# One adaLN block at each of four edges of a decoder trunk, in place of ten pieces of each mixing part

## The reference

```python
mod = (jax.nn.silu(c) @ w_ada + b_ada).reshape(B, N_SUB, 3, D_MODEL)
m_shift, m_scale, m_gate = mod[:, :, 0], mod[:, :, 1], mod[:, :, 2]

def sub_in(t, i):
    return rmsnorm(t, norm_pre[i]) * (1.0 + m_scale[:, i, None]) + m_shift[:, i, None]

def sub_out(t, y, i, res):
    return t + res * m_gate[:, i, None] * rmsnorm(y, norm_post[i])

x = sub_out(x, swiglu(sub_in(x, 0), ffn_up[0], ffn_down[0]), 0, FFN_RES)
h = sub_in(x, 1)
pa, pb, pg = split_cols(h @ w_in, [A_COLS, B_COLS, 2 * D_MODEL])
...
x = sub_out(x, merged, 1, 1.0)
x = sub_out(x, swiglu(sub_in(x, 2), ffn_up[1], ffn_down[1]), 2, FFN_RES)
```

## Time and profile before

| | |
|---|---|
| runs | 2221.89, 2221.23 and 2217.05 us, median 2221.23 |
| the profiled execution | 2214.12 us |
| its span on the core | 2212.4 us |
| mean granted PE clock | 0.937 |
| PE busy | 2025.4 us, 92% |
| DVE, ACT busy | 57%, 43% |
| DMA, mean over the span | 160 GB/s |

### The profile page before, as it was taken

One profiled execution on the slowest core, in us unless ns is written; L12 is line 12 of the kernel. 1 busy time (PEld: TensorE's weight loads), 2 busy tenths in 40 slices (PEclk: granted clock), 3 DMA queues, 4 the chain that ended last, 5 costly groups with the idle time before them and its releaser, 6 DMA issues.

```text
span 2212.4 us, 44807 instructions
## 1 busy us (share of the span) xinstructions
PE 2025.4 (92%) x19104; PEld 1831.7 (83%) x19104; DVE 1256.2 (57%) x2161; ACT 954.3 (43%) x1872; POOL 4.8 (0%) x30
## 2 busy tenths in 40 slices
PE   6999989889999997899989998988899989879997
PEld 4899868778877877789989996888898878668997
DVE  3554455656456555677566645455654655558853
ACT  4333464444466413433454445433445752253343
POOL 0000000000000000000000000000000000000000
PEclk8999999999999887899999999888999988789998
DMA  7787755556555536697646655434545444167762
GB/s 255 219 233 200 196 143 153 160 143 183 132 161 149 155 83 149 165 254 221 193 121 181 181 174 142 127 107 129 134 108 143 108 120 124 51 160 220 229 192 93
DMA packets 579797, 353.33 MB, mean 160 GB/s; under 512 B 43989, under 2 KB 539639, under 8 KB 578047
## 3 DMA queue, kind: packets, MB, share of 16 engines
q1 hardware_dynamic: 490634, 302.74, 48.6%
q10 hardware_dynamic: 88964, 47.74, 8.7%
HBM read 332.27 MB, written 18.50 MB: 159 GB/s over the span
## 4 chain that ended last, share of the span: by engine, by line
PE 74%; DVE 9%; DMA 7%; ACT 6%; issue 3%; ACTq 2%; SPq 0%; DVEq 0%
PE bank L879 70%; DMA ring<-in_w_ada 3%; DMA ring<-in_ffn_up 2%; DVE ring_r L731 2%; DVE far L1904 1%; ACT w_hi_r L723 1%; DVE big L1904 1%; PE bank L644 1%; PE bank L657 1%; ACTq L570 1%; DVE big L1907 1%; ACTq L625 1%; ACT h L1448 1%; DVE big L606 1%; DVE far L1907 1%
## 5 line engine op out<-in xcount | busy, mean ns | idle before, releaser
L879 PE MATMUL bank<-big_r,w_hi_r 128*128 128x264 f32 x4160 | 1082.1, 294 | 54.4 <-DVE h_r L1904 41.0
L879 PE MATMUL bank<-big_r,ring_r 128*128 128x264 f32 (+1 forms) x3456 | 999.1, 289 | 0.0
L879 PEld LDWEIGHTS bank<-big_r,w_hi_r 128*128 128x128 f32 x4160 | 754.6, 193 | 127.1 <-issue 90.9
L879 PE MATMUL bank<-h_r,w_hi_r 128*128 128x264 f32 x2752 | 802.0, 291 | 0.0
L731 DVE TENSOR_TENSOR ring_r<-ring,w_hi_r 128x1024 fp32r<-128x1024 f32 (+2 forms) x440 | 524.4, 1195 | 477.6 <-ACT w_hi_r L723 473.7
L879 PEld LDWEIGHTS bank<-big_r,ring_r 128*128 128x128 f32 (+1 forms) x3456 | 668.5, 193 | 1.0
L723 ACT CAST w_hi_r<-ring 128x1024 fp32r<-128x1024 f32 (+2 forms) x440 | 452.1, 1028 | 498.5 <-PE bank L879 288.1
L879 PEld LDWEIGHTS bank<-h_r,w_hi_r 128*128 128x128 f32 x2752 | 535.5, 195 | 1.1
L879 PE MATMUL bank<-big,far 64*64 64x64 f32 (+2 forms) x1440 | 158.9, 268 | 0.0
L879 PEld LDWEIGHTS bank<-big,far 64*64 64x64 f32 (+1 forms) x1440 | 124.5, 144 | 7.2 <-issue 6.7
L879 PE MATMUL bank<-ring,c 128*32 128x256 f32 x1152 | 95.7, 411 | 27.8 <-DMA ring<-in_w_ada 19.7
(11 more groups left out here) (287 smaller groups left out, 1924.9 us busy)
## 6 DMA issues: line engine op xcount, KB each, us to landing
ring<-in_ffn_up SPq DMA_DIRECT2D x176, 512.0 KB, 4.7
ring<-in_w_in SPq DMA_DIRECT2D x148, 512.0 KB, 3.9
ring<-in_w_ada SPq DMA_DIRECT2D x144, 512.0 KB, 4.0
ring<-in_ffn_down SPq DMA_DIRECT2D x64, 512.0 KB, 3.8
far<-in_state_gdn_ssm ACTq DMA_DIRECT2D x28, 512.0 KB, 6.0
ring<-in_ffn_down SPq DMA_DIRECT2D x32, 384.0 KB, 3.2
ring<-in_w_out SPq DMA_DIRECT2D x16, 512.0 KB, 4.7
out_sample_gdn_ssm<-far ACTq DMA_DIRECT2D x16, 512.0 KB, 4.2
```

The lines of the kernel that those rows point to most:

```text
L879: return pe.matmul(out, lhsT, rhs, start=start, stop=stop)
```

## The change

Four blocks move to four edges: (0,0), (0,1), (0,2) and (1,0). At each, three units stand on PE right behind the first mean (`edge_begins`), the fourth behind the fifth product of the second mean, and the sum piece behind the second mean. ACT copies `ada_rows` between the seventh and the eighth square and `modv` after `normalise`. Both mixing parts lose ten pieces: layer 0 leaves out turns 1, 2, 6, 11, 16, 21, 26, 31, 36, 41 and 46 (turn 1 had none before), and layer 1 keeps those of turns 0, 2, 5, 7, 10 and so on, up to 72. The means go from bank 7, where the units write, to bank 0, and wait there for the eviction of the output tile before. In the plan the next part's first two tiles take the two oldest slots ahead of the edge's units. `weight_plan` is written anew and, but for this, gives the same order.

```diff
 def mix_pieces(l, turn):

     if l == 0:
-        return 1 if turn != 1 else 0
-    return 1 if turn % 2 == 0 or turn in (3, 5) else 0
+        return 0 if turn in (1, 2, 6, 11, 16, 21, 26, 31, 36, 41, 46) else 1
+    return 1 if turn % 5 in (0, 2) and turn < 75 else 0
+
+
+def edge_pieces(l, sub):
+
+    return ADA_UNITS + 1 if (l, sub) in ((0, 0), (0, 1), (0, 2), (1, 0)) else 0
...
+def ring_slots(plan, in_mixing, edges):

     ended, count = [-1] * RING, [0] * RING
-    slot, before, nth_load = [], [], []
-    for n, (_, kind, _) in enumerate(plan):
+    slot, before, nth_load = ([0] * len(plan) for _ in range(3))
+    order = list(range(len(plan)))
+    for n in edges:
+        order[n:n + ADA_UNITS + 2] = [n + ADA_UNITS, n + ADA_UNITS + 1, *range(n, n + ADA_UNITS)]
+    for n in order:
         own = range(RING)
         if n in in_mixing:
-            own = (RING - 1,) if kind == "ada" else range(RING - 1)
+            own = (RING - 1,) if plan[n][1] == "ada" else range(RING - 1)
         s = min(own, key=lambda s: ended[s])
...
-                    def mean_square(bank=7, buf=h):
-
+                    def mean_square(buf=h, sub=None):
+
+                        m, fill = (l, sub) if sub != 2 else (l - 1, 2), sub is not None
                         for k in range(NT):
                             pe.wait_ge(sq_ready.sem, sq_ready.next(pe))
-                            i = mm(banks[bank][:, 0:T], mean_all[:, :], buf[:, k, :], k == 0, k == NT - 1)
+                            i = mm(banks[0][:, 0:T], mean_all[:, :], buf[:, k, :], k == 0, k == NT - 1)
+                            if fill and k == 4 and edge_pieces(*m):
+                                ada_pieces(1)
                         i.then_inc(ss_done.sem, ss_done.one())
+                        if fill and edge_pieces(*m):
+                            ada_pieces(1)
+
+                    def edge_begins(sub):
+                        if edge_pieces(l, sub):
+                            ada_pieces(ADA_UNITS - 1)
...
-                        if l == 0:
-                            pe.wait_ge(ada_taken.sem, ada_taken.nth((ADA_FFN, ADA_MIX + ADA_FFN)[i_ffn]))
+                        pe.wait_ge(out_taken.sem, out_taken.at(base + 5))
                         mean_square()
+                        edge_begins(2 * i_ffn)
...
-                    def square_input(start=False):
+                    def square_input(start=False, m=None):
                         for j in range(NT):
                             if j == 0 or not start:
                                 act.wait_ge(x_ready.sem, x_ready.next(act))
                             act.activation(h[:, j, :], xT[:, j, :], ACT.Square).then_inc(sq_ready.sem, sq_ready.one())
+                            if m and j == 6 and edge_pieces(*m):
+                                ada_pieces(ADA_UNITS)
+                        if start:
+                            ada_pieces(ADA_UNITS)
+                        normalise()
+                        if m and edge_pieces(*m):
+                            ada_pieces(1)
```

More of the change, by code:

```diff
@@ L131, in mix_pieces, with units, edge @@
     if l == 0:
[L132 to L133 removed]
+        return 0 if turn in (1, 2, 6, 11, 16, 21, 26, 31, 36, 41, 46) else 1
+    return 1 if turn % 5 in (0, 2) and turn < 75 else 0
+def edge_pieces(l, sub):
+    return ADA_UNITS + 1 if (l, sub) in ((0, 0), (0, 1), (0, 2), (1, 0)) else 0
 def weight_plan():
[L138 to L139 removed]
+    steps = iter([key for m, b in ada_order() for key in ada_units(m, b, b + 1) + [None]])
+    def units(n):
+        return [key for key in itertools.islice(steps, n) if key]
+    plan, in_mixing, edges = units(ADA_FIRST * (ADA_UNITS + 1)), set(), []
+    def edge(l, sub):
+        if edge_pieces(l, sub):
+            edges.append(len(plan))
+        plan.extend(units(edge_pieces(l, sub)))
@@ L150, in weight_plan @@
[L150 to L154, removed]
+            plan += [(l, "down0", 3 * o + n) for n in range(3)] + units(ffn_pieces(l, 0, FT + o))
+        edge(l, 0)
+        first = len(plan)
         for t in range(TURNS):
             plan += [(l, *k) for k in TILES[t:t + 1] if t > 1] or [(l, *k) for k in TILES[0:2] if t == 0]
[L157 to L160, removed]
@@ L161, in weight_plan @@
-        assert piece % (ADA_UNITS + 1) == 0
+            plan += units(mix_pieces(l, t))
         in_mixing |= set(range(first, len(plan)))
         plan += [(l, "out", n) for n in range(NT)]
+        edge(l, 1)
         for t in range(FT):
[L165 to L168, removed]
+            plan += [(l, "up1", 2 * t), (l, "up1", 2 * t + 1)] + units(ffn_pieces(l, 1, t))
@@ L169, in weight_plan @@
         plan += [(l, "down1", n) for n in range(3 * NT)]
-    return plan, in_mixing
-def ring_slots(plan, in_mixing):
+        edge(l, 2)
+    assert not list(steps)
+    return plan, in_mixing, edges
+def ring_slots(plan, in_mixing, edges):
     ended, count = [-1] * RING, [0] * RING
-    slot, before, nth_load = [], [], []
-    for n, (_, kind, _) in enumerate(plan):
+    slot, before, nth_load = ([0] * len(plan) for _ in range(3))
[3 more added lines that the diff above has]
+    for n in order:
@@ L694, in build @@
         xs_rows = part(big, WORK + 2176, P)
-        plan, in_mixing = weight_plan()
-        slot, before, nth_load = ring_slots(plan, in_mixing)
+        plan, in_mixing, edges = weight_plan()
+        slot, before, nth_load = ring_slots(plan, in_mixing, edges)
         where = {key: n for n, key in enumerate(plan)}
```

44 lines of the change are left out of this document (16 added, 28 removed).

## The result

The changed kernel runs at 2233.69 us, the median of 13 runs (2221.14 to 2242.88), against 2221.23 before (13 runs, 2208.47 to 2235.53): a ratio of 1.0055, with a 95% interval of 1.0033 to 1.0078. It is slower, by some 12 us. A second series of the same kernel gave 2234.45 us and 1.0064 (1.0043 to 1.0085).

What follows compares the result with a forecast made beforehand. It took PE, busy 92% of the span, as the bound. Layer 0 -4.2, layer 1 -3.5 and edges +2.0 gave -5.7 us; from the median 2221.2 that is 2215.5, stated as 2216, range 2205 to 2229.

Steps and rivals of the forecast that it cites:

- the half clock takes it all, and more: Rival, chance 0.20: fewer pieces leave PE idle before DVE-bound products; layer 0 +0.6, layer 1 +2.5, edges +5.2, 2229.5 us.
- I take two of the three as fallen: Layer 0's mixing part: clock falls at two of three gaps, +9.6 against -13.8 gained; net -4.2, bounds -13.8 and +0.6.
- the three gaps: Layer 0's PE waits before products of turns 8, 23 and 38; a fallen clock costs 6.1, 4.8 and 3.5 us.
- The wait at turn 31 only moves: Rival, chance 0.20: in layer 0 later work inherits the wait, so the 6.6 us are not won; +0.9, 2222 us.
- Layer 1, -3.5: Layer 1's mixing part: ten pieces fewer, 5.2 us, two thirds counted as saved; bounds -5.2 and +2.5.
- turn 29, with a wait past 2 us: Layer 1's mixing part: a PE wait near this turn grows past 2 us; if the clock falls there, +6.
- The edges, +2.0: The four edges together: 0.4, 1.0, -0.1 and 0.4, plus 0.3 for the third load; upper bound 5.2.
- the third load: Edge (0,0): the third unit's load on SP's queue may land just in time; 0 to 1 us.
- a sign of being wrong: At an edge: the prediction is wrong if PE waits there for ring<-in_w_ada for over 1 us.
- The 0.57 us a unit: PE time of one adaLN unit at the full clock; with a 0.3 us sum piece, a block is 2.6 us.
- the 5.22 us wait of turn 31: Layer 0: a unit waits for the copy of modv; the wait goes and t_blocks' products start earlier, gain 6.6 us.
- the comparison of the two mixing parts: Before the change, layer 1 with 35 pieces fewer is 2.3 us longer, 569.0 against 566.7, at clock 0.90 against 0.94.

Runs made afterwards that it cites:

- l0_only: Half of the change: blocks at edges (0,0) and (0,1) with layer 0's skips, the rest as in the kernel before; 2232.66 us, 1.0045.
- after_fill_l1: The changed kernel with matmuls that nobody reads ahead of PE's waits before the pairs' products, in layer 1's mixing part alone; 2217.21 us, 0.9980.
- edges_eased: The changed kernel with two units, not one, within the second mean and the copy of ada_rows behind the second normalise; 2235.98 us, 1.0084.
- l1_only: Half of the change: blocks at edges (0,2) and (1,0) with layer 1's skips, the rest as in the kernel before; 2227.71 us, 1.0026.
- before_fill_l1: The kernel before with matmuls that nobody reads ahead of PE's waits before the pairs' products, in layer 1's mixing part alone; 2202.78 us, 0.9926.
- rep_after: The changed kernel run once more, unedited, for a second profile; 2234.45 us, 1.0064.
- late_skips: The changed kernel with the turns without pieces moved: odd turns 45 to 63 in layer 0, late even turns in layer 1; 2224.17 us, 1.0020.
- two_restored: The changed kernel with pieces at turns 6 and 21 of layer 0 again and none at turns 51 and 56; 2225.35 us, 1.0013.
- the halves: The two runs l0_only and l1_only, each with one half of the change; 2232.66 us and 2227.71 us.
- more_fill: The kernel before with unread matmuls ahead of the pairs' products, t_blocks waits and some second means, and at mixing parts' entries; 2204.74 us, 0.9910.
- after_fill: The changed kernel with matmuls that nobody reads ahead of PE's waits before the pairs' products, in both layers; 2205.25 us, 0.9932.
- rep_before: The kernel before run once more, unedited, for a second profile; 2217.22 us, 0.9994.
- the two with filling: The kernel before with unread matmuls ahead of the pairs' products, in both layers (2195.46 us) or in layer 1 alone (2202.78 us).

## Why the prediction was wrong

It forecast 2216 us and a gain; the kernel is 12 us slower. It had the mechanism, as a rival with a chance of 0.20 ("the half clock takes it all, and more", 2229.5 us), and still undersized it.

**Layer 0, "I take two of the three as fallen", with a bound of +0.6.** This step failed. Five profiles with the change's skips in this layer and nothing filled there (the change twice, l0_only, after_fill_l1 and edges_eased) have a mixing part of 573.3 to 586.3 us, 579.3 on average. Four with the pattern of before (before twice, l1_only, before_fill_l1) have 566.4 to 571.0, 567.7 on average: +11.6 us where I had -4.2. Profiles are single executions, and by the timed runs the whole change costs 12 to 15, so this part is likely less than 11.6. The trace has 24 products of the projection for each turn, so it tells where each turn starts. The same five profiles against the same four, on average, in us, beside what the sum had (two thirds of the price at the three gaps):

| turns of layer 0's part | forecast | measured |
|---|---|---|
| 0 to 5 | -3.0 | -2.6 |
| 6 to 9, with the gap of turn 8 | +4.1 | +5.5 |
| 10 | 0 | +2.9 |
| 11 to 16 | -1.5 | -1.5 |
| 17 to 20 | 0 | +3.2 |
| 21 to 23, with the gap of turn 23 | +3.2 | +5.0 |
| 24 to 30 | -1.2 | +0.1 |
| 31 | -6.6 | -6.4 |
| 32 to 35 | 0 | +4.4 |
| 36 to 39, with the gap of turn 38 | +1.9 | +3.7 |
| 40 to 56 | -1.1 | -0.8 |
| 57 to the end | 0 | -2.0 |

The gains came nearly as forecast. Two things failed.

First, the odds at the three gaps, some 5 us. The price of a fallen clock was right on the whole: with all three fallen the sum has +14.0, and 14.2 is measured. But all three fell, in each of the five profiles, at waits of 2.9 to 3.2 us. I had worked out 2.3 to 2.65 us before turn 8, and held 2.5 us for a wait that leaves the clock alone, from one row. The same trace has a row against it, a unit that waits 2.35 us in layer 0, with the window behind it:

```profile
397.24 0.64 PE L879 MATMUL bank<-ring,c 128*32 128x256 f32 x8 [2.35 <-DMA ring<-in_w_ada]
397.20:403.20 6.00, 5.40 (x33) 0.72 0.57 166
```

Over all twenty profiles, of the waits of 2.0 to 3.0 us with PE at the full clock ahead of them, 186 of 234 were followed by the half clock within 4 us; of those from 1.25 to 1.5 us, 121 of 269; of those under 1 us, 117 of 732. (Many are the same place in several profiles.) I had taken a handful of rows of one execution for a rule.

Second, waits that were not in the sum: 10.5 us at turns 10, 17 to 20 and 32 to 35, put at nothing. The sum counted the places where a piece was taken out. But with the pattern, every sum and every fourth unit moved to another turn: a load came late at turn 10 (2.49 us), a copy of ada_rows came to stand behind the gather of turn 18 (2.70 us), and behind turn 31, whose 6.4 us were won, the products of t_blocks now wait (1.87 us in the first profile) and run at half. "The wait at turn 31 only moves", a rival with 0.20, was right in kind: the wait itself is gone, and part of what it gave is lost within four turns.

**Layer 1, -3.5.** Nine profiles with the change's skips and nothing filled in this layer average 574.0 us, three with the old ones 570.5: +3.5. The waits before turns 20 and 23 grew from 4.79 and 2.88 to 5.23 and 3.22 us. What counts more is the clock behind waits that hardly differ: it fell behind turn 14's, of 1.28 us, in three of the nine (5.1 us each) and behind turn 29's, of 1.7 us, in four (4.7 us each in rep_after and edges_eased), and held at both in the three with the old pattern. The prediction had named turn 29, with a wait past 2 us; the wait stayed, and the clock fell all the same in some executions.

**The edges, +2.0.** In the two profiles of the change, against the mean of the two of before: (0,0) +0.9 and +0.3, (0,2) +0.2, (1,0) +3.6 and +2.3, and from layer 0's mixing part to FFN 1's first product, with (0,1), +1.1 and +1.8. Together +5.8 and +4.5, about the upper bound of 5.2. The term that failed is the third load, "0 to 1 us": it waits 1.7 us at (0,0) and 2.65 at (1,0), over the 1 us that the prediction named as a sign of being wrong. I had put the loads in their order on SP's queue and not followed that the LoRA loads ahead of them wait for the last down tile. Edges_eased, which takes that wait and the copy between the squares away, still has 16.65 us, 0.5 above before, at (0,0).

**What was right.** The 0.57 us a unit; the 5.22 us wait of turn 31 gone, and 6.4 us won there against 6.6; that the waits of turns 8 and 23 would grow to over 2 us; and the comparison of the two mixing parts in the earlier trace rows, which said that fewer pieces are not less time, and which the sum should have been made to obey. It needed no mechanism: layer 1's pattern had lost 2.3 us with 35 pieces less, and the change takes layer 0 a step towards it.

**What the timed runs say of the clock.** Each timed run has its mean granted clock on record. Over 122 runs of the kernel before in the later series it goes from 0.926 to 0.942, and the time falls by 1.6 us for each 0.001 more. The change's 25 runs have 0.925 on average. By that line they should take 2234.5 us, and they take 2233.4. So the 12 us go wholly with the clock: when the kernel before is granted as little, it is as slow. The same holds for late_skips, two_restored and the halves to 3.3 us. It is a relation and not an experiment, and no law for all kernels: more_fill lies 9 us above the line, after_fill and after_fill_l1 5 us below it.

**What stays open.** Restoring two pieces gives 9 us, and neither PE work in their place nor in the waits behind them does. So, as far as these runs tell, the two skips cost by what else they bring: the loads' times, and the turns in which sums and copies fall. Which of these was not told apart, and the pieces taken out at turns 51 and 56 instead were not tried alone. Nor is it known why filling layer 0 helps only when layer 1 is filled as well; that a gain in layer 0 is given back in layer 1 by the clock is shown in one profile, and not for the runs.

## What to carry to other kernels

Where PE's clock falls behind waits, small work that fills a wait is worth more than its own time: look first at the same stage with and without it, and if the leaner one isn't faster, don't price its removal at its duration. Pieces strewn by a pattern are one chain: taking out every fifth moves all the rest, so list for before and after which turn each sum, copy and load falls in, against the DMA issues on the same queues. And judge such a change by timed runs; single profiles of one kernel here had a stage at 573 and at 586 us. Set each run's mean clock beside its time: it tells whether a loss goes with the clock before any place is looked for.

## What the runs showed of the hardware that was not expected

Matmuls that nobody reads, ahead of waits, took 24 us, 1.1%, off the kernel before (2195.46 us against 2219.23 in the same series), the fastest version of all tried. Waits of 1.25 to 1.5 us were in 121 of 269 cases followed by the half clock.

And the same instructions behind the same wait, started earlier or later, kept the clock in one profile and lost it in another. Turn 14 of layer 1, in the two profiles of the changed kernel, each with its window:

```profile
1469.04 0.70 PE L878 MATMUL bank<-far,ones_half 128*128 128x256 f32 x2 [1.28 <-DVE big L1916]
1469.00:1475.00 6.00, 5.96 (x56) 0.66 0.30 85
1458.94 0.70 PE L878 MATMUL bank<-far,ones_half 128*128 128x256 f32 x2 [1.28 <-DVE big L1916]
1458.90:1464.90 6.00, 5.96 (x83) 1.00 0.31 87
```

Layer 1's mixing part with the change's skips took 569.9 to 584.5 us over nine profiles, without an edit in it. FFN 1 of layer 0, from its first product to its first mean, took 230.4 to 235.7 us in four profiles of kernels that have it as before (before, rep_before and the two with filling).
